# RMS norms of a YOCO decoder step: squares summed on TensorE without GpSimd, and 1/sqrt split between ScalarE and VectorE

## What is computed

```
def rms_norm(x, g):
    y = xf * lax.rsqrt(jnp.mean(xf * xf, axis=-1, keepdims=True) + EPS)
    return (y * g).astype(x.dtype)
...
for layer in range(DEPTH):
    if layer == N_A_LAYERS:
        ckv_new, kr_new = kv_side(x, ...)          # two norms: kv_in_g on x, kv_g on the latent
    h = rms_norm(x, pre_mix_g[layer])
    m = sgu_mixer(h, ...) or mla_mixer(h, ...)     # one more norm inside each (sgu_g, q_g)
    x = x + rms_norm(m, post_mix_g[layer])
    h = rms_norm(x, pre_ffn_g[layer])
    f = conv_ffn(h, ...)
    x = x + rms_norm(f, post_ffn_g[layer])
```

## Time and profile before

| | before |
|---|---|
| device time, median of 3 runs | 1741.18 us (1739.67 to 1741.36) |
| profiled execution, first to last instruction | 1737.2 us |
| around it: median less span | 3.98 us |
| mean granted TensorE clock, share of full | 0.951 |
| PE busy | 1584.2 us, 91% |
| DVE busy | 989.3 us, 57% |
| ACT busy | 644.5 us, 37% |
| POOL busy | 225.6 us, 13% |
| chain that ended last | PE 83%, DVE 7%, ACT 4%, issue 2% |

### The profile page before, as it was taken

The page is one execution under the profiler, slowest core; times in us unless marked ns, Lnnn a source line. Parts: engine busy times, 40 slices in busy tenths (PEclk is TensorE's granted clock), DMA queues, the critical chain, the costliest instruction groups (busy, mean ns, idle before and its releaser), DMA issues.

```text
span 1737.2 us, 32432 instructions
## 1 busy us (share of the span) xinstructions
PE 1584.2 (91%) x11908; PEld 1441.5 (83%) x11908; DVE 989.3 (57%) x1652; ACT 644.5 (37%) x1038; POOL 225.6 (13%) x388
## 2 busy tenths in 40 slices
PE   4897999977999999995997999899995999999997
PEld 3797998977999999995984666544594999999996
DVE  3343664247888884336545656415636888886333
ACT  3444443234222223335515555423435222223333
POOL 0000000002322221002002111000002223322000
PEclk9898999999999999998997999897998999999998
DMA  6132222321232322332213434210021333332331
GB/s 195 51 95 61 74 72 66 94 73 49 86 96 88 93 80 84 90 102 97 74 35 96 115 107 108 79 33 7 1 77 33 89 93 90 91 93 68 97 92 57
DMA packets 250794, 138.16 MB, mean 80 GB/s; under 512 B 28412, under 2 KB 246578, under 8 KB 250696
## 3 DMA queue, kind: packets, MB, share of 16 engines
q1 hardware_dynamic: 242080, 126.20, 25.2%
q0 software_dynamic: 4256, 8.89, 1.6%
q10 hardware_dynamic: 4376, 2.00, 0.5%
HBM read 133.74 MB, written 3.67 MB: 79 GB/s over the span
## 4 chain that ended last, share of the span: by engine, by line
PE 83%; DVE 7%; ACT 4%; issue 2%; ACTq 0%; DVEq 0%
PE psum L574 65%; PE psum L915 3%; PE psum L901 2%; DVE x L1505 2%; PE psum L937 2%; PE psum L1002 2%; PE psum L1028 2%; DVE ut L1502 1%; PE psum L1027 1%; PE psum L1045 1%; PE psum L694 1%; PE psum L1037 1%; DVE xl L1490 1%; ACT wh L1090 1%; ACT lat_h L1359 1%
## 5 line engine op out<-in xcount | busy, mean ns | idle before, releaser
L574 PE MATMUL psum<-xh,wh 128*128 128x260 f32 x2112 | 436.0, 288 | 48.8 <-DVE xl L1490 33.6
L1469 DVE TENSOR_TENSOR wl<-ws,wh 128x1024 fp32r<-128x1024 f32 x221 | 270.7, 1226 | 366.4 <-ACT wh L1090 364.4
L574 PE MATMUL psum<-xh,wl 128*128 128x260 f32 x2112 | 431.1, 286 | 0.0
L574 PE MATMUL psum<-xl,wh 128*128 128x260 f32 x2112 | 431.0, 286 | 0.0
L1090 ACT ACTIVATE wh<-ws 128x1024 fp32r<-128x1024 f32 x221 | 233.3, 1056 | 527.7 <-PE psum L574 527.7
L574 PEld LDWEIGHTS psum<-xh,wh 128*128 128x128 f32 x2112 | 332.4, 193 | 53.8 <-issue 33.5
L574 PEld LDWEIGHTS psum<-xh,wl 128*128 128x128 f32 x2112 | 331.5, 192 | 0.0
L574 PEld LDWEIGHTS psum<-xl,wh 128*128 128x128 f32 x2112 | 331.4, 192 | 0.0
L574 PE MATMUL psum<-acth,wh 128*128 128x260 f32 x704 | 142.4, 283 | 0.0
L574 PE MATMUL psum<-acth,wl 128*128 128x260 f32 x704 | 141.6, 282 | 0.0
L574 PE MATMUL psum<-actl,wh 128*128 128x260 f32 x704 | 141.3, 282 | 0.0
(11 more groups left out here) (248 smaller groups left out, 2312.0 us busy)
## 6 DMA issues: line engine op xcount, KB each, us to landing
ws<-in_w_up SPq DMA_DIRECT2D x88, 512.0 KB, 3.8
ws<-in_w_in_a SPq DMA_DIRECT2D x32, 512.0 KB, 4.0
ws<-in_w_down SPq DMA_DIRECT2D x32, 384.0 KB, 3.4
cn<-in_cache_ckv SPq DMA_DIRECT2D x96, 128.0 KB, 2.0
ws<-in_w_down SPq DMA_DIRECT2D x32, 320.0 KB, 3.1
ws<-in_w_out_a SPq DMA_DIRECT2D x16, 512.0 KB, 4.0
cn<-in_cache_ckv POOLq DMA_DIRECT2D x32, 128.0 KB, 2.4
ws<-in_w_o SPq DMA_DIRECT2D x8, 512.0 KB, 4.5
```

Source lines behind the costliest of these rows:

```text
L574: mm = pe.matmul(psum[:, 2 * slot + b, 0:HB], w, r[:, k, b * HB:(b + 1) * HB], start=st, stop=en)
L1469: dve.tensor_tensor(wl[:, slot2, :], ws[:, slot4, :], f32(wh[:, slot2, :]), ALU.subtract).then_inc(w_low, 1)
```

## The change

Two things are changed.

1. For x1, x2 and x3 no engine adds squares any more. PE multiplies ones by the square of each tile, right after that tile's products, and accumulates in PSUM: 8 pairs of matmuls in place of 2 pairs. A new semaphore `sq_summed` tells ACT that a slot of `sq` is free. GpSimd loses all of its 18 additions.
2. For all 11 norms ACT computes sqrt(mean + eps) in one activation and DVE takes the reciprocal of the 128x520 result in place. DVE waits for the reciprocal before it goes on; the semaphore `ln_done` becomes `sd_done`.

The core of the diff (a second run of replaced call names, the same for each norm, is left out):

```diff
+ON_PE = ("x1", "x2", "x3")
...
-                for t in range(KD):
-                    add_squares(pool, f"x{1 + 2 * l}", t, t % 2)
...
-            for t in range(KD):
-                add_squares(pool, "x2", t, t % 2)
...
-            def two_units(n, rh, rl, ready):
+            def two_units(n, rh, rl, ready, sums=None):
...
+                    if sums:
+                        sum_squares(sums, k)
+
+            def sum_squares(name, t):
+
+                g = GI[name]
+                if t == 0:
+                    wait(pe, sd_done, g)
+                pe.wait_ge(sq_done, SQB[name] + t + 1)
+                for b in range(2):
+                    mm = pe.matmul(psum[:, 6 + b, 0:HB], ones[:, :], sq[:, t % 2, b * HB:(b + 1) * HB], start=(t == 0), stop=(t == KD - 1))
+                if t == KD - 1:
+                    mm.then_inc(ss_done, 1)
+                else:
+                    mm.then_inc(sq_summed, 1)
...
-                two_units(U_UP[l], xh, xl, [(xl_ready, KD * p)])
-                rms("x1" if l == 0 else "x3")
+                two_units(U_UP[l], xh, xl, [(xl_ready, KD * p)], sums="x1" if l == 0 else "x3")
...
-            two_units(U_KV, xkh, xkl, [(xkl_ready, 0)])
-            rms("x2")
+            two_units(U_KV, xkh, xkl, [(xkl_ready, 0)], sums="x2")
...
-            def rms(name, dst):
+            def deviation(name, dst):
                 g = GI[name]
 
-                act.activation(warm[:, :], ones[:, 0:1], ACT.Ln)
+                act.activation(warm[:, :], ones[:, 0:1], ACT.Sqrt)
                 act.wait_ge(ss_done, g + 1)
-                act.activation(halves(dst[:, :]), psum[:, 6:8, 0:HB], ACT.Ln, bias=eps[:, 0:1], scale=1.0 / GROUPS_SQ[g][2]).then_inc(ln_done, 1)
-                act.wait_ge(ln_done, g + 1)
-                act.activation(dst[:, :], dst[:, :], ACT.Exp, scale=-0.5).then_inc(r_ready, 1)
+                act.activation(halves(dst[:, :]), psum[:, 6:8, 0:HB], ACT.Sqrt, bias=eps[:, 0:1], scale=1.0 / GROUPS_SQ[g][2]).then_inc(sd_done, 1)
...
+                elif name in ON_PE:
+                    act.wait_ge(sq_summed, (KD - 1) * ON_PE.index(name) + t - 1)
...
+            def rms(name, dst):
+
+                dve.wait_ge(sd_done, GI[name] + 1)
+                dve.reciprocal(dst[:, :], dst[:, :]).then_inc(r_ready, 1)
+                dve.wait_ge(r_ready, GI[name] + 1)
...
-                dve.wait_ge(r_ready, GI[["", "m_sgu", "m_ffn0", "m_attn", "m_ffn1"][p]] + 1)
+                rms(["", "m_sgu", "m_ffn0", "m_attn", "m_ffn1"][p], r2)
...
-            dve.wait_ge(r_ready, GI["x2"] + 1)
+            rms("x2", r1)
...
-            dve.wait_ge(r_ready, GI["kv"] + 1)
+            rms("kv", r2)
...
-            dve.wait_ge(r_ready, GI["cq"] + 1)
+            rms("cq", r2)
```

More of the change, by code:

```diff
@@ L77 @@
 MB = {"m_sgu": 0, "m_ffn0": KD, "m_attn": 2 * KD, "m_ffn1": 3 * KD}
-SQA = {n: sum(c - 2 for _, c, _ in GROUPS_SQ[:i]) for i, (n, _, _) in enumerate(GROUPS_SQ)}
+ON_PE = ("x1", "x2", "x3")
+SQA = {n: sum(c - 2 for m, c, _ in GROUPS_SQ[:i] if m not in ON_PE) for i, (n, _, _) in enumerate(GROUPS_SQ)}
 SQB = {n: sum(c for _, c, _ in GROUPS_SQ[:i]) for i, (n, _, _) in enumerate(GROUPS_SQ)}
@@ L278, in trunk @@
         w_high, w_low, mm_done = S("w_high"), S("w_low"), S("mm_done")
-        sq_done, sq_added, ss_done, ln_done, r_ready = S("sq_done"), S("sq_added"), S("ss_done"), S("ln_done"), S("r_ready")
+        sq_done, sq_added, sq_summed, ss_done, sd_done, r_ready = (S(n) for n in (
+            "sq_done", "sq_added", "sq_summed", "ss_done", "sd_done", "r_ready"))
         x_new, u_mul, xh_ready, xl_ready, xkh_ready, xkl_ready = (S(n) for n in (
@@ L607, in rms @@
                 before = sqa[:, :] if n > 2 else sq[:, 0, :]
-                wait(pe, ln_done, g)
+                wait(pe, sd_done, g)
                 for b in range(2):
@@ L654, in _ @@
             pe.wait_ge(d_gate, 16)
-            pe.wait_ge(ln_done, 1)
+            pe.wait_ge(sd_done, 1)
             for g in range(GROUPS):
@@ L707, in _ @@
             pe.wait_ge(mix_read, KG)
-            pe.wait_ge(ln_done, GI["v"] + 1)
+            pe.wait_ge(sd_done, GI["v"] + 1)
             for g in range(4):
@@ L838, in _ @@
             pe.wait_ge(rotk_step, 2)
-            pe.wait_ge(ln_done, GI["cq"] + 1)
+            pe.wait_ge(sd_done, GI["cq"] + 1)
             for h in range(H):
@@ L1176, in _ @@
                 if u == 0:
-                    rms("x0", r1)
+                    deviation("x0", r1)
                 value_tile(0, u)
@@ L1192, in gate_tile @@
                     ahead(U_U, 4, i, u)
-                    rms("v", r2)
+                    deviation("v", r2)
                     act.wait_ge(rT_done, 1)
@@ L1235, in _ @@
             wo(3)
-            rms("m_sgu", r2)
+            deviation("m_sgu", r2)
             update(1)
@@ L1247, in tile @@
                     if first:
-                        rms("x1" if l == 0 else "x3", r1)
+                        deviation("x1" if l == 0 else "x3", r1)
                     q, j = 4 * i + u, 2 * i + u // 2
@@ L1287, in mlp @@
                     down(3, e, guard=True)
-                rms(g, r2)
+                deviation(g, r2)
             mlp(0)
@@ L1294, in _ @@
             ahead_static(U_KV)
-            rms("x2", r1)
+            deviation("x2", r1)
             for t in range(KC):
@@ L1304, in _ @@
             ahead_static(U_DQ)
-            rms("kv", r2)
+            deviation("kv", r2)
             for t in range(KQ):
@@ L1313, in _ @@
             act.wait_ge(ckt_ready, KC)
-            rms("cq", r2)
+            deviation("cq", r2)
             for j in range(4):
@@ L1453, in _ @@
             ahead_static(U_O + KD - 1)
-            rms("m_attn", r2)
+            deviation("m_attn", r2)
             update(3)
@@ L1528, in value_tile @@
                 if first:
-                    dve.wait_ge(r_ready, 1)
+                    rms("x0", r1)
                 wait(dve, z_done, j - 1)
@@ L1560, in gate_tile @@
                 if first:
-                    dve.wait_ge(r_ready, GI["v"] + 1)
+                    rms("v", r2)
                 dve.scalar_tensor_tensor(out=vsn[:, bass.ds(j, 1), :].rearrange("p o t -> p (o t)"),
@@ L1630, in tile @@
                     if first:
-                        dve.wait_ge(r_ready, GI["x1" if l == 0 else "x3"] + 1)
+                        rms("x1" if l == 0 else "x3", r1)
                         dve.wait_ge(zpad, 1 + l)
```

## The result

The changed kernel takes 1746.39 us in the median of 6 runs (1744.71 to 1750.66), the kernel before 1739.43 us (1738.12 to 1741.36, 6 runs beside them). The ratio is 1.0036, with an interval from 1.0024 to 1.0049: slower by 0.36%, or 6.3 us (0.0036 x 1739.43; the plain difference of the medians is 7.0). The profiled execution of the changed kernel is the slowest of its six, 1750.66 us with a span of 1749.0 us, so its span is read by stages and not as a whole.

What follows compares the result with a forecast made beforehand. Bound by a chain over PE (83%), except at norms where PE waits for DVE and ACT, and updates bound by DVE. With R = 3.3: 29.7 - 23.5 + 0.8 = 7.0 us on 1741.2, 1748 us; range 1737 to 1765.

Steps and rivals of the forecast that it cites:

- What R is: R, the time of DVE's reciprocal on 128x520: taken as 3.3 us, between 0.70 and 6.4 us.
- The sum is 9R - 23.5 us: Whole kernel's change with reciprocal time R, plus 2(R - 2.9) where R is above 2.9; zero at R = 2.6 us.
- Six norms, 6R - 11.1 us: At x0, v, m_sgu, m_ffn0, m_attn, m_ffn1, where PE waits: 1.98 us behind Ln become reciprocal time R + 0.13.
- Three updates, 3R - 13.7 us: Updates up to the x1, x2, x3 factors: 3R + 77.2 us against 90.9 before, R being the reciprocal's time.
- My other bound: In the updates, PE at the low clock throughout: its 18.6 us for eight tiles would be 37.2; not taken.
- kv and cq, 2(R - 2.9) us: Two norms where PE has cover: no cost if reciprocal time R is under 2.9 us, otherwise R - 2.9 late each.
- The Exp load: New table load ahead of the first Exp over the samples, taken to be on the chain: 1.3 us.
- A drain at a switch of tables: The skill's 1380 ns beside each table load, 1.38 us more gain at nine norms, some 12 us; not counted.
- Eight steps an element: Rival: DVE's reciprocal works each element eight times, about 4.5 us on 128x520; 20 us slower, 1761 us; chance 0.30.
- The plain reciprocal: Rival: DVE's reciprocal costs a plain instruction, 0.7 us; 17 us faster, 1724 us; chance 0.20.
- The update that doesn't get shorter: Rival: DVE's long adds in the updates have another cause than GpSimd, PE's sums only hide; 1754 us; chance 0.05.

Runs made afterwards that it cites:

- part one alone: Kernel before, with the squares of x1, x2, x3 summed on PE and none on GpSimd, Ln and Exp kept: 1736.54 us, ratio 0.9966.

## Why the prediction was right

Forecast were 1748 us, 7.0 us slower, and a gain in the updates that is eaten by nine reciprocals on the path; measured were 1746.39 us, 6.3 us slower, and the trace shows that mechanism. The closeness of the number is in part luck, as the first and the fourth step show. By its own steps:

**"What R is": right in size, by a lucky choice.** I took 3.3 us, about halfway between what the 128x1 row and the 8x1 row said; it is 3.40. Half of the 11 ns is 5.5, which I rounded to 5; with 5.5 it would have been 3.6 us and a forecast of 1751. Neither row carried the answer. On 128x1 the reciprocal and a multiply both take 153 ns, though on 128x520 they take 3402 and 430, so that row shows no price of an element; and the 11 ns of the 8x1 row are not one either, since 520 of them would be 5.7 us. The two widths measured above give 6.25 ns a column. Had the element been worked in one step, the forecast's sign would have been wrong, and no row of the kernel before could have warned of it. The chances of 0.43, 0.30 and 0.20 said as much.

**"The sum is 9R - 23.5 us": shown at three values of R**, in the table above. That R decides the sign, and that it does so near 2.6 us, is the part of the forecast that was worked out and not chosen; a straight line between the two measured points around it turns at 2.7 us.

**Six norms, 6R - 11.1 us: right.** With R = 3.40 that is 9.3 us; 6 x 1.49 = 8.9 were measured.

**Three updates, 3R - 13.7 us: right in sum, with an error in the clock.** It gives -3.5 us; -3.8 were measured, as 1.0, 1.7 and 1.05 us. PE was the slower engine with a pair every 2.31 us (2.33 forecast), adds of `x` took 0.70, and there was no pause between sums. But I carried the low clock over from before, 3.6, 5.5 and 5.9 us, of which half is lost: 1.8, 2.8 and 3.0 us. It lasted 5.8, 3.9 and 5.4 us, so the losses were 2.9, 2.0 and 2.7 us. Update 1 therefore came out 1.0 us longer than forecast, update 2 0.9 shorter and update 3 0.4 shorter; by the forecast update 1 gained most, and it gained least. Both sets of losses add up to 7.6 us: that the three updates together are right is luck. My other bound, PE at the low level throughout, did not come.

**kv and cq, 2(R - 2.9) us: right in size.** 1.0 us by R = 3.40, measured 1.3: at kv PE waits 0.58 us for DVE's `cqr`, and with it its last sum for cq starts 0.8 us later behind x2's first use (37.88 before, 38.68 after); at cq PE waits 0.52 us for DVE's `qn`:

```profile
848.84 0.51 PE L556 MATMUL psum<-xh,wh 128*128 128x260 f32 x2 [0.58 <-DVE cqr L1727]
...
867.59 3.39 DVE L1477 RECIPROCAL r<-r 128x520 f32<-128x520 f32 x1
...
871.02 1.30 DVE L1751 TENSOR_TENSOR qn<-psum,r 128x520 f32<-128x520 f32 x2
...
871.77 0.51 PE L556 MATMUL psum<-cqh,wh 128*128 128x260 f32 x2 [0.52 <-DVE qn L1751]
```

**The Exp load, 1.3 us: wrong, it is 0.** I read that the Exps are on the chain there and priced the load in full. The chain names the activation, not what ACT did ahead of it: ACT had 1.54 us of idle time before the first Exp, and the load fits into it. This step was settled by the two rows shown above, without a run.

**A drain at a switch of tables: not in these traces.** Behind the square root of x1 the next load starts at 411.69, 0.03 us after the root's end (410.97 + 0.69), and the load is 1.28 us (1283 ns in the mean). The Trainium skill, ScalarE: Activation LUTs, section "What ACT_TABLE_LOAD costs", is borne out in its 1283 ns and not in its 1380 ns of drain.

**The rivals.** Eight steps an element (1761 us): refuted by the 6.25 ns a column; the time lies outside too. The plain reciprocal (1724 us): refuted, and the 21.6 us gained with a plain instruction of 0.43 us in its place, where the formula has 19.6, show that its price was worked out rightly. The update that doesn't get shorter (1754 us): refuted by the adds of 0.70 us, by the kernel without GpSimd's additions and by part one alone, which is 5.9 us faster.

What stays open is why the low clock lasts longer in one update and shorter in another, the rest of the 6.6 us between the parts one by one and together, and the few us by which the attention stage differs from one execution to the next at a differing granted clock.

## What to carry to other kernels

An instruction's price at one column says nothing of its price at 520: where a forecast hangs on it and no row shows the width, solve for the value at which the sign turns (here R = 2.6 us), say so, and measure that one first. Work that is taken from one engine to free another has to be cheap where it lands: without GpSimd's additions DVE was 6.5 us faster an update, and the sums took more than half of it back on PE, until the form of the operands made them nearly four times cheaper. A load of a function table need not be removed to leave the path: with Ln and Exp kept and the load issued earlier, the kernel took 1725 us, and the change that saves the loads by a reciprocal 1746. And before a new load or wait is priced because its activation is on the chain, look at the idle time that this activation already had ahead of it.

## What the runs showed of the hardware

- DVE's reciprocal in float32 takes 3402 ns on 128x520, 1777 on 128x260 and 153 on 128x1, so 6.25 ns a further column; a tensor-scalar instruction on 128x520 takes 430 ns.
- An add of two SBUF tiles on DVE (0.70 us) takes up to 1.85 us when GpSimd adds beside it.
- A pair of matmuls by a matrix of ones on 128x260 takes 0.88 us of PE in float32 and 0.24 in float32r.
- Ln followed by Exp cost two table loads of 1283 ns each, here at every norm; a load starts 0.01 to 0.03 us behind the activation before it (409.09 to 409.10 before, 411.66 to 411.69 after).
- Behind PE's start in an update the clock stayed at 0.50 for 3.6, 5.5 and 5.9 us in the kernel before and for 5.8, 3.9 and 5.4 us in the changed one, where PE has more to do in all three: longer in one update, shorter in two.
